# Dilated attention: two units' score products issued in turn from the two halves of the array's rows

## The chip, the cores and the metric

The kernel runs on one core of a Trainium2 chip. The metric is the device time of one execution in microseconds (us). Three runs of the kernel before took 2505.32, 2506.44 and 2511.6 us; the median is 2506.44 us.

## What is computed

The program is two transformer blocks over 512 tokens of width 1024, in float32. The change touches the dilated attention of the second one: three groups of heads (dilations 1, 4 and 16), 16 heads of 64 dimensions each.

```python
proj = (h @ w_in).reshape(B, S, N_GROUPS_2, 3, N_HEADS_2, HEAD_DIM)
for g, (window, dil) in enumerate(DILATED_PATTERNS):      # (128, 1), (512, 4), (2048, 16)
    q = partial_rotary(proj[:, :, g, 0], pos)
    k = partial_rotary(proj[:, :, g, 1], pos)
    v = proj[:, :, g, 2]
    o, lse = dilated_band_attention(q, k, v, dil, window // dil)
...
s = jnp.einsum('bcnihd,bcnjhd->bcnhij', qb, kb).astype(jnp.float32) * (D ** -0.5)
s = jnp.where(valid[None, None, :, None, :, :], s, NEG_INF)
m = jnp.max(s, axis=-1, keepdims=True)
p = jnp.exp(s - m)
den = jnp.sum(p, axis=-1, keepdims=True)
o = jnp.einsum('bcnhij,bcnjhd->bcnihd', p / den, vb.astype(jnp.float32))
```

The three outputs are merged by a softmax over their log-denominators and multiplied by `a_w_out`.

## The kernel before

The mixer is worked through in six passes, `v` = 0 to 5: eight heads of one group each, the groups in the order 1, 2, 0, 1, 2, 0. Tokens are four tiles (`t`) of 128. A **unit** is what fits one PSUM bank of scores, 128 queries by 512 scores: four heads by one key tile in groups 1 and 2 (8 units in a pass), two heads by two key tiles in group 0 (16 units, passes 2 and 5). TensorE does three things for a unit:

- `scores`: four products of 128 x 128, queries by keys, into bank 6 for even units and bank 7 for odd ones. They contract over the 64 dimensions of a head. Even heads lie on partitions 0 to 63 of `dqT` and `dkT` and odd heads on 64 to 127; `first_head` gives all heads of an even unit from the lower half and all of an odd unit from the upper one.
- `turn_probs`: four transposes of the probabilities into bank 4 or 5.
- `times_values`: four products with 64 columns of values, into `G`.

Between them VectorE scales and masks the scores into `dsc` (L2895), reduces the maximum (L2901) and negates it (L2902); ScalarE takes the exponentials (L2115) and copies the transposed probabilities from PSUM to `dPT` (L2103). Both take their work strictly in the order of the code. VectorE also takes a finished tile's output out of `G` (`tile_end`, L2882, or the merge of the three groups in passes 2 and 5) behind its odd units, and rotates the next pass's queries and keys.

In passes 0 to 4 units are laid between the steps of the next pass's projection: `project(v + 1, i)`, i = 0 to 11, each 24 matmuls of 512 columns (L872 to L874), which in turn need weights that ScalarE splits into a high part (L1726) and GpSimd into a low part (L3028). One unit follows each of the steps 1 to 8, or two in group 0 (`units_after`). In pass 5 there is no next projection: one unit lies inside step 11 of its own projection, one behind it, and the others between steps of the output product (`AO_STEPS`), where the first four steps are the transposes at L1417.

A unit is issued as `unit(u)`: `turn_probs(u)`, `scores(u + 2)`, `times_values(u - 1)`, with `scores(0)` and `scores(1)` ahead of the first. `scores(u)` waits until VectorE has read unit `u - 2` (`at_read`), `turn_probs(u)` until its probabilities are there (`at_prob`), `times_values(u)` until ScalarE's copy is (`at_copied`).

Of the kernel before, what the change touches and what calls it, by code (L numbers as in the profile page):

```python
# [28 lines left out]
P = 128  # L29
# [6 lines left out]
DH = 64  # L36
# [53 lines left out]
def two_blocks_kernel(nc, a):  # L90
# [155 lines left out]
    dqT = at("dqT", AR + 16, [P, 4, T])  # L246
# [234 lines left out]
    def first_head(q, heads):  # L481
        return q if heads == 4 else 4 * (q // 2) + q % 2
# [30 lines left out]
    def units_after(v):  # L513
        return [0] + [2 if group_of(v) == 0 else 1] * 8
# [347 lines left out]
    def _(pe):  # L862
# [586 lines left out]
        for v in range(6):  # L1449
            g = group_of(v)  # L1450
            hu = 2 if g == 0 else 4
            per_tile = HH // hu
            units = NT * per_tile

            def scores(u):
                t, q = divmod(u, per_tile)
                if u >= 2:
                    pe.wait_ge(at_read, unit0 - 32 + u - 1)
                for e in range(hu):
                    h = first_head(q, hu) + 2 * e  # L1460
                    rows = slice(DH * (h % 2), DH * (h % 2) + DH)
                    q_ = dqT[rows, h // 2, t * P:(t + 1) * P]
                    keys = ([t, t - 1] if t else [0, 0]) if g == 0 else [t]
                    for z, kt in enumerate(keys):
                        o = (e * len(keys) + z) * P
                        last = pe.matmul(SB[u % 2][:, o:o + P], q_, dkT[rows, h // 2, kt * P:(kt + 1) * P],  # L1466
                                         start=True, stop=True)
                last.then_inc(at_scores, 1)

            def turn_probs(u):  # L1470
                pe.wait_ge(at_prob, unit0 + u + 1)
                if u >= 2:
                    pe.wait_ge(at_copied, unit0 + u - 1)
                for c in range(4):
                    last = pe.transpose(TB[u % 2][:, c * P:(c + 1) * P], dsc[:, u % 3, c * P:(c + 1) * P], ident)
                last.then_inc(at_turned, 1)

            def times_values(u):
                t, q = divmod(u, per_tile)
                pe.wait_ge(at_copied, unit0 + u + 1)  # L1480
                if q == 0:
                    pe.wait_ge(at_done, NT * (v + 1) + t - 1)
                for e in range(hu):
                    h = first_head(q, hu) + 2 * e
                    keys = ([t, t - 1] if t else [0, 0]) if g == 0 else [t]
                    for z, kt in enumerate(keys):
                        o = (e * len(keys) + z) * P
                        last = pe.matmul(G[t % 2][:, h * DH:(h + 1) * DH], dPT[:, u % 3, o:o + P],  # L1488
                                         dV[:, v % 2, kt, h * DH:(h + 1) * DH], start=(z == 0), stop=(z == len(keys) - 1))
                if q == per_tile - 1:  # L1490
                    last.then_inc(at_out, 1)

            def unit(u):
                turn_probs(u)
                if u + 2 < units:
                    scores(u + 2)
                if u >= 1:
                    times_values(u - 1)

            if v < 5:  # L1500
                project(v + 1, 0)
            if v < 5:
                pe.wait_ge(turn_free, chunk[0])
                pe.wait_ge(dl_evac, 12 * (v + 1))
            else:

                pe.wait_ge(turn_free, chunk[0] - 2)
                pe.wait_ge(dl_evac, 12 * (v + 1) - 2)
            scores(0)
            scores(1)  # L1510
            u = 0
            if v < 5:
                for i in range(1, 9):
                    project(v + 1, i)
                    for _ in range(units_after(v)[i]):
                        unit(u)
                        u += 1

                def values_end():
                    times_values(units - 1)  # L1520
                    pe.wait_ge(at_copied, unit0 + units)
                project_values(v + 1, 9, values_end)
            else:
                def first_unit():
                    pe.wait_ge(turn_free, chunk[0])
                    unit(0)

                project(v, 11, first_unit)
                unit(1)
                pe.wait_ge(dl_evac, 12 * (v + 1))  # L1530
                for u in range(2, units):
                    first = sum(AO_STEPS[:u])
                    for f, k in ao_steps[first:first + AO_STEPS[u]]:
                        out_step(f, k)
                    unit(u)
                rest = ao_steps[sum(AO_STEPS):]
                for f, k in rest[:4]:
                    out_step(f, k)
                times_values(units - 1)
                for f, k in rest[4:]:  # L1540
                    out_step(f, k)
            unit0 += units
# [1681 lines left out]
```

## Time and profile before

| | |
|---|---|
| median of three runs | 2506.44 us |
| span of the profiled execution | 2509.7 us |
| TensorE busy | 2449.8 us, 98% of the span |
| VectorE, ScalarE, GpSimd busy | 39%, 39%, 36% |
| granted TensorE clock, mean of the span | 0.993 |
| the six passes, in the trace | 870 to 1437 us |

The span is the time from the first to the last instruction of one profiled execution; no separate time of that execution is shown, and its span lies inside the range of the three runs. Busy time of TensorE counts records of matmuls, which overlap, so 98% says that it seldom waits, not that it works at its peak.

### The profile page before, as it was taken

How to read it: one execution, taken by the hardware profiler on the slowest of the kernel's cores; microseconds unless marked ns; L12 is line 12 of the kernel's file. 1: busy time of each engine (PE TensorE's matmuls, PEld its weight loads, DVE VectorE, ACT ScalarE, POOL GpSimd, SP SyncE). 2: the span in 40 equal slices, each digit the busy share in tenths (PEclk: the TensorE clock that was granted, in tenths of full speed). 3: DMA queues.
4: the chain of work that ended last, by engine and by line, in shares of the span. 5: the costliest groups of instructions: out<-in, count | busy, mean ns of one | idle time of the engine just before them, and what ended most of it. 6: DMA issues, size and time to landing. Idle time of an engine off the chain costs nothing.

```text
span 2509.7 us, 31117 instructions
## 1 busy us (share of the span) xinstructions
PE 2449.8 (98%) x11644; PEld 1930.5 (77%) x11644; DVE 984.9 (39%) x1627; ACT 974.6 (39%) x1611; POOL 906.0 (36%) x757
## 2 busy tenths in 40 slices
PE   7999999999998999999999999999999999999998
PEld 6776786545556998899987878888777777788887
DVE  3276445878884233353335621111311113211113
ACT  3343433656653343343343442222343343422223
POOL 4442141424432433323332154455332221544552
PEclk9999999999999999999999999999999999999999
DMA  5421136899982423311223123323322111233322
GB/s 172 164 67 51 34 125 243 320 380 390 383 321 101 151 70 104 98 51 52 84 91 96 34 84 102 101 94 90 101 102 68 67 51 34 84 101 101 100 85 92
DMA packets 210220, 316.17 MB, mean 126 GB/s; under 512 B 20624, under 2 KB 140176, under 8 KB 200256
## 3 DMA queue, kind: packets, MB, share of 16 engines
q1 hardware_dynamic: 202368, 301.89, 35.4%
q0 software_dynamic: 7744, 12.76, 1.5%
q8 instruction: 76, 1.25, 0.2%
q14 instruction: 32, 0.26, 0.0%
HBM read 300.81 MB, written 22.71 MB: 129 GB/s over the span
## 4 chain that ended last, share of the span: by engine, by line
PE 85%; issue 4%; ACT 3%; DMA 3%; DVE 2%; POOL 2%; SPq 0%; DVEq 0%; ACTq 0%; POOLq 0%
PE bank L872 21%; PE bank L874 20%; PE bank L873 20%; PE bank L1309 4%; PE bank L1102 3%; DMA w_ring<-in_w_gate 2%; PE bank L1466 2%; POOL w_low L3028 2%; PE bank L1488 2%; PE bank L1122 2%; PE bank L1293 2%; PE bank L1288 2%; PE bank L911 2%; ACT w_high L1726 1%; PE bank L1112 1%
## 5 line engine op out<-in xcount | busy, mean ns | idle before, releaser
L3028 POOL TENSOR_TENSOR w_low<-raw,w_high 128x512 fp32r<-128x512 f32 x568 | 748.0, 1349 | 1268.4 <-ACT w_high L1726 1236.5
L872 PE MATMUL bank<-h_high,w_high 128*128 128x512 f32 x1088 | 434.6, 399 | 2.3 <-DVE h_low L2293 2.3
L874 PE MATMUL bank<-h_high,w_low 128*128 128x512 f32 x1088 | 424.6, 390 | 0.0
L873 PE MATMUL bank<-h_low,w_high 128*128 128x512 f32 x1088 | 423.9, 390 | 0.0
L1726 ACT ACTIVATE w_high<-raw 128x2048 fp32r<-128x2048 f32 x145 | 277.0, 1910 | 295.6 <-PE bank L874 283.1
L872 PE MATMUL bank<-w_high,h_high 128*128 128x512 f32 (+2 forms) x832 | 332.5, 400 | 10.6 <-ACT qk L2061 5.5
L874 PE MATMUL bank<-w_high,h_low 128*128 128x512 f32 (+2 forms) x832 | 312.6, 376 | 0.0
L873 PE MATMUL bank<-w_low,h_high 128*128 128x512 f32 (+2 forms) x832 | 312.3, 375 | 0.0
L872 PEld LDWEIGHTS bank<-h_high,w_high 128*128 128x128 f32 x1088 | 204.4, 188 | 50.3 <-DVE h_low L2293 6.1
L874 PEld LDWEIGHTS bank<-h_high,w_low 128*128 128x128 f32 x1088 | 204.2, 188 | 43.5
L873 PEld LDWEIGHTS bank<-h_low,w_high 128*128 128x128 f32 x1088 | 204.6, 188 | 38.9
L872 PEld LDWEIGHTS bank<-w_high,h_high 128*128 128x128 f32 x832 | 205.3, 247 | 26.2 <-ACT qk L2061 5.8
L873 PEld LDWEIGHTS bank<-w_low,h_high 128*128 128x128 f32 x832 | 206.6, 248 | 10.5
L874 PEld LDWEIGHTS bank<-w_high,h_low 128*128 128x128 f32 x832 | 204.9, 246 | 12.6
L2545 DVE TENSOR_TENSOR up_low<-w_ring,up_high 128x2048 fp32r<-128x2048 f32 x70 | 160.1, 2288 | 39.2 <-ACT up_high L1980 36.9
L2276 DVE TENSOR_TENSOR X<-bank,X 128x512 f32<-128x512 f32 x96 | 65.8, 690 | 235.6 <-PE bank L874 235.4
L2273 DVE TENSOR_TENSOR gu<-silu,bank 128x512 f32<-128x512 f32 x44 | 30.3, 688 | 321.4 <-ACT silu L2173 321.4
L2173 ACT ACTIVATE silu<-bank 128x512 f32<-128x512 f32 x44 | 26.3, 599 | 333.0 <-PE bank L874 333.0
L1980 ACT ACTIVATE up_high<-w_ring 128x2048 fp32r<-128x2048 f32 x70 | 133.9, 1915 | 33.3 <-DMA w_ring<-in_w_gate 30.7
L872 PE MATMUL bank<-w_high,act_high 128*128 128x512 f32 x352 | 136.9, 389 | 0.0
L873 PE MATMUL bank<-w_low,act_high 128*128 128x512 f32 x352 | 136.9, 389 | 0.0
L874 PE MATMUL bank<-w_high,act_low 128*128 128x512 f32 x352 | 136.9, 389 | 0.0
(374 smaller groups left out, 3501.7 us busy)
## 6 DMA issues: line engine op xcount, KB each, us to landing
raw<-in_ffn_w_gu SPq DMA_DIRECT2D x88, 512.0 KB, 4.5
raw<-in_a_w_in SPq DMA_DIRECT2D x72, 512.0 KB, 4.8
w_ring<-in_w_gate SPq DMA_DIRECT2D x35, 1024.0 KB
w_ring<-in_w_up SPq DMA_DIRECT2D x35, 1024.0 KB
w_ring<-in_w_down SPq DMA_DIRECT2D x35, 1024.0 KB
raw<-in_ffn_w_down SPq DMA_DIRECT2D x40, 512.0 KB, 4.6
raw<-in_w_in SPq DMA_DIRECT2D x34, 512.0 KB, 4.7
raw<-in_b_w_in SPq DMA_DIRECT2D x24, 512.0 KB, 4.8
```

Source lines behind the costliest of these rows:

```text
L872: pe.matmul(out, sta[0], mov[0], start=start, stop=False)
L873: pe.matmul(out, sta[0], mov[1], start=False, stop=False)
L874: return pe.matmul(out, sta[1], mov[0], start=False, stop=stop)
L911: last = pe.transpose(TB[m % 2][:, t * P:(t + 1) * P], src, ident)
L1102: pe.matmul(S3[u % deep][:, 0:(qt + 1) * P], q_[rows, h // 2, qt * P:(qt + 1) * P], k_[rows, h // 2, 0:(qt + 1) * P], start=True, stop=False)
L1122: last = pe.matmul(G[qt % 2][:, h * DH:(h + 1) * DH], pt_[:, u % deep, kt * P:(kt + 1) * P], v_[:, kt, h * DH:(h + 1) * DH], start=(kt == ...
L1309: last = pe.matmul(G[2 + half][0:R, :], het[:, c, :], w[:, c, 512 * half:512 * half + 512], start=(c == 0), stop=(c == 1))
L1726: act.activation(w_high[:, slot, :], raw[:, slot, :], ACT.Copy).then_inc(high_done, 1)
L1980: act.activation(up_high[:, b, :, FE * q:FE * q + FE], ring[:, q, :].rearrange("p (k n) -> p k n", k=KD), ACT.Copy).then_inc(m_high, 1)
L2276: return dve.tensor_tensor(out=out, in0=x, in1=y, op=ALU.add)
L2545: dve.tensor_tensor(out=up_low[:, b, :, FE * q:FE * q + FE], in0=ring[:, q, :].rearrange("p (k n) -> p k n", k=KD), in1=up_high[:, b, :, F ...
L3028: last = pool.tensor_tensor(out=w_low[:, slot, cols], in0=raw[:, slot, cols], in1=w_high[:, slot, cols].bitcast(F32), op=ALU.subtract)
```

## The change

Units are taken by twos. `scores(u)`, now for even `u` only, issues the eight products of units `u` and `u + 1` in turn: one of the even unit (lower half of the rows, bank 6), one of the odd unit (upper half, bank 7), and so on, and waits for both units before. `pair(u)` is two `turn_probs`, the eight score products of the next two units, and two `times_values`, that of `u - 1` and, new in its place, that of `u`. In passes with one unit after each projection step the pair follows every second step. The work of the other engines and its order are the same.

```diff
             def scores(u):
-                t, q = divmod(u, per_tile)
                 if u >= 2:
-                    pe.wait_ge(at_read, unit0 - 32 + u - 1)
-                for e in range(hu):
-                    h = first_head(q, hu) + 2 * e
-                    rows = slice(DH * (h % 2), DH * (h % 2) + DH)
-                    q_ = dqT[rows, h // 2, t * P:(t + 1) * P]
-                    keys = ([t, t - 1] if t else [0, 0]) if g == 0 else [t]
-                    for z, kt in enumerate(keys):
-                        o = (e * len(keys) + z) * P
-                        last = pe.matmul(SB[u % 2][:, o:o + P], q_, dkT[rows, h // 2, kt * P:(kt + 1) * P],
-                                         start=True, stop=True)
-                last.then_inc(at_scores, 1)
+                    pe.wait_ge(at_read, unit0 - 32 + u)
+                for i in range(4):
+                    for w in (u, u + 1):
+                        t, q = divmod(w, per_tile)
+                        keys = ([t, t - 1] if t else [0, 0]) if g == 0 else [t]
+                        e, z = divmod(i, len(keys))
+                        h = first_head(q, hu) + 2 * e
+                        rows = slice(DH * (h % 2), DH * (h % 2) + DH)
+                        last = pe.matmul(SB[w % 2][:, i * P:(i + 1) * P], dqT[rows, h // 2, t * P:(t + 1) * P],
+                                         dkT[rows, h // 2, keys[z] * P:(keys[z] + 1) * P], start=True, stop=True)
+                        if i == 3:
+                            last.then_inc(at_scores, 1)
...
-            def unit(u):
+            def pair(u):
                 turn_probs(u)
+                turn_probs(u + 1)
                 if u + 2 < units:
                     scores(u + 2)
                 if u >= 1:
                     times_values(u - 1)
+                times_values(u)
...
-                    for _ in range(units_after(v)[i]):
-                        unit(u)
-                        u += 1
+                    u = sum(units_after(v)[:i + 1])
+                    if u % 2 == 0:
+                        pair(u - 2)
...
-                def first_unit():
+                def first_units():
                     pe.wait_ge(turn_free, chunk[0])
-                    unit(0)
-
-                project(v, 11, first_unit)
-                unit(1)
+                    pair(0)
+
+                project(v, 11, first_units)
                 pe.wait_ge(dl_evac, 12 * (v + 1))
-                for u in range(2, units):
+                for u in range(2, units, 2):
                     first = sum(AO_STEPS[:u])
-                    for f, k in ao_steps[first:first + AO_STEPS[u]]:
+                    for f, k in ao_steps[first:first + AO_STEPS[u] + AO_STEPS[u + 1]]:
                         out_step(f, k)
-                    unit(u)
+                    pair(u)
```

On TensorE, in pass 2 behind projection step 2, the rows before are these. Banks 4 and 5 take the turned probabilities (`dsc`), 6 and 7 the scores (`dkT`, `dqT`), 0 and 1 are `G`.

```order
L1475 MATMUL bank4<-cst_50,dsc_184 128x128 x4
L1466 MATMUL bank6<-dkT_180,dqT_179 128x128 x4
L1488 MATMUL bank0<-dV_182,dPT_185 128x64 x4
L1475 MATMUL bank5<-cst_50,dsc_184 128x128 x4
L1466 MATMUL bank7<-dkT_180,dqT_179 128x128 x4
L1488 MATMUL bank0<-dV_182,dPT_185 128x64 x4
```

In the change the same place reads so (the lines have moved by one).

```order
L1476 MATMUL bank4<-cst_50,dsc_184 128x128 x4
L1476 MATMUL bank5<-cst_50,dsc_184 128x128 x4
L1466 MATMUL bank6<-dkT_180,dqT_179 128x128
L1466 MATMUL bank7<-dkT_180,dqT_179 128x128
L1466 MATMUL bank6<-dkT_180,dqT_179 128x128
L1466 MATMUL bank7<-dkT_180,dqT_179 128x128
L1466 MATMUL bank6<-dkT_180,dqT_179 128x128
L1466 MATMUL bank7<-dkT_180,dqT_179 128x128
L1466 MATMUL bank6<-dkT_180,dqT_179 128x128
L1466 MATMUL bank7<-dkT_180,dqT_179 128x128
L1489 MATMUL bank0<-dV_182,dPT_185 128x64 x8
```

The number of products is the same; six runs of one kind of work have become three, and banks 6 and 7 alternate.

The second place is in pass 5 on TensorE, behind projection step 11: the rows before, from unit 1 to unit 3, with the transposes of the output product (L1417) between them.

```order
L1475 MATMUL bank5<-cst_50,dsc_184 128x128 x4
L1466 MATMUL bank7<-dkT_180,dqT_179 128x128 x4
L1488 MATMUL bank0<-dV_182,dPT_185 128x64 x4
L1417 MATMUL bank2<-cst_50,xn_92 128x128 x4
L1417 MATMUL bank3<-cst_50,xn_92 128x128 x4
L1475 MATMUL bank4<-cst_50,dsc_184 128x128 x4
L1466 MATMUL bank6<-dkT_180,dqT_179 128x128 x4
L1488 MATMUL bank0<-dV_182,dPT_185 128x64 x4
L1417 MATMUL bank2<-cst_50,xn_92 128x128 x4
L1417 MATMUL bank3<-cst_50,xn_92 128x128 x4
L1475 MATMUL bank5<-cst_50,dsc_184 128x128 x4
L1466 MATMUL bank7<-dkT_180,dqT_179 128x128 x4
```

And in the change, from the last matmul of step 11:

```order
L874 MATMUL bank3<-w_high_88,h_low_91 128x512
L1417 MATMUL bank2<-cst_50,xn_92 128x128 x4
L1417 MATMUL bank3<-cst_50,xn_92 128x128 x4
L1417 MATMUL bank2<-cst_50,xn_92 128x128 x4
L1417 MATMUL bank3<-cst_50,xn_92 128x128 x4
L1476 MATMUL bank4<-cst_50,dsc_184 128x128 x4
L1476 MATMUL bank5<-cst_50,dsc_184 128x128 x4
L1466 MATMUL bank6<-dkT_180,dqT_179 128x128
L1466 MATMUL bank7<-dkT_180,dqT_179 128x128
```

Unit 1 has moved ahead, into the middle of step 11; no unit stands between step 11 and the transposes, nor between the first and the second two of them.

## Rows read from the trace of the kernel before

**Rows 1.** The page, busy time and share of each engine.

```profile
PE 2449.8 (98%) x11644; PEld 1930.5 (77%) x11644; DVE 984.9 (39%) x1627; ACT 974.6 (39%) x1611; POOL 906.0 (36%) x757
```

**Rows 2.** Passes 2 and 5: busy us (instructions) of each engine, granted clock, DMA.

```profile
1054.00:1168.00 114.00, 114.00 (x643) 108.65 (x643) 60.28 (x113) 45.09 (x102) 31.36 (x25) 1.00 0.21 65
...
1339.00:1437.00 98.00, 93.68 (x552) 78.39 (x550) 61.98 (x116) 38.35 (x97) 19.96 (x16) 0.97 0.19 55
```

**Rows 3.** Score line L1466 by source: ns min/median/max; idle us, times.

```profile
L1466 PE MATMUL bank<-dkT,dqT x512: 272/272/579, 871.1 to 1420.9; 64*128 64x128 f32 x171
...
  issue: 10.2, 57
```

**Rows 4.** Timeline, TensorE, pass 0: start us, us, work; one unit between projection steps.

```profile
894.42 0.60 PE L1475 MATMUL bank<-cst,dsc 128*128 128x128 f32 x4
894.95 1.16 PE L1466 MATMUL bank<-dkT,dqT 64*128 64x128 f32 x8
896.04 1.10 PE L1488 MATMUL bank<-dV,dPT 128*128 128x64 f32 x8
896.95 0.60 PE L872 MATMUL bank<-w_high,h_high 128*128 128x512 f32 x1
897.39 0.40 PE L873 MATMUL bank<-w_low,h_high 128*128 128x512 f32 x1
897.63 0.40 PE L874 MATMUL bank<-w_high,h_low 128*128 128x512 f32 x1
```

**Rows 5.** Timeline, TensorE, pass 2: two units next to each other.

```profile
1072.29 0.60 PE L1475 MATMUL bank<-cst,dsc 128*128 128x128 f32 x4
...
1077.82 0.40 PE L873 MATMUL bank<-w_low,h_high 128*128 128x512 f32 x1
```

**Rows 6.** Timeline, pass 1, scores 0 and 1 next to each other: loads and products.

```profile
964.27 1.52 PEld L1466 LDWEIGHTS bank<-dkT,dqT 64*128 64x128 f32 x16 [0.35 <-issue]
964.27 1.71 PE L1466 MATMUL bank<-dkT,dqT 64*128 64x128 f32 x16
```

**Rows 7.** Timeline, TensorE, pass 1: one unit between projection steps.

```profile
978.71 0.60 PE L1475 MATMUL bank<-cst,dsc 128*128 128x128 f32 x4
...
981.56 0.39 PE L873 MATMUL bank<-w_low,h_high 128*128 128x512 f32 x1
```

**Rows 8.** Timeline, pass 0: end of step 7, rotation, GpSimd's low part, start of step 9.

```profile
927.68 0.40 PE L874 MATMUL bank<-w_high,h_low 128*128 128x512 f32 x1
...
930.00 2.52 DVE L2273 TENSOR_TENSOR rot<-qk,cst 128x256 f32<-128x256 f32 x4
...
930.69 5.82 POOL L3028 TENSOR_TENSOR w_low<-raw,w_high 128x512 fp32r<-128x512 f32 x4 [3.92 <-ACT w_high L1726]
...
933.88 1.51 DVE L2276 TENSOR_TENSOR qk<-rot 128x256 f32<-128x256 f32 x1
...
936.57 0.63 PE L872 MATMUL bank<-w_high,h_high 128*128 128x512 f32 x1
```

**Rows 9.** Timeline, start of pass 5: turning of unit 0, last exponential of unit 1, turning of unit 3.

```profile
1347.29 0.63 PE L1475 MATMUL bank<-cst,dsc 128*128 128x128 f32 x4 [0.57 <-ACT dsc L2115]
...
1348.07 0.49 ACT L2115 ACTIVATE dsc<-dsc,nmx 128x256 f32<-128x256 f32 x1
...
1360.98 0.66 PE L1475 MATMUL bank<-cst,dsc 128*128 128x128 f32 x4 [2.12 <-ACT dsc L2115]
```

**Rows 10.** Windows, columns as in rows 2: a stretch of pass 5.

```profile
1361.60:1368.40 6.80, 6.80 (x24) 5.93 (x24) 3.18 (x8) 2.47 (x8) 0.00 (x0) 0.50 0.49 154
```

**Rows 11.** Timeline, pass 2: values of unit 3, GpSimd, last exponential of unit 7.

```profile
1084.84 1.10 PE L1488 MATMUL bank<-dV,dPT 128*128 128x64 f32 x8
...
1086.47 5.47 POOL L3028 TENSOR_TENSOR w_low<-raw,w_high 128x512 fp32r<-128x512 f32 x4 [6.04 <-ACT w_high L1726]
...
1092.77 0.50 ACT L2115 ACTIVATE dsc<-dsc,nmx 128x256 f32<-128x256 f32 x1
```

**Rows 12.** Timeline, VectorE, pass 5: a finished output group is added.

```profile
1369.77 0.69 DVE L2276 TENSOR_TENSOR X<-bank,X 128x512 f32<-128x512 f32 x1 [4.53 <-PE bank L874]
```

More of the change, by code:

```diff
@@ L1509, in _ @@
             scores(0)
-            scores(1)
-            u = 0
             if v < 5:
```

## The prediction, made before the changed kernel ran

> **What bounds the kernel now.** I read the page first: TensorE is busy for 98% of the span and every other engine for less than 40% [rows 1], so only time on TensorE counts, unless the change makes it wait. The windows say the same of the passes: in pass 2 it is busy for all 114 us at a clock of 1.00, with VectorE at 60 and ScalarE at 45 us; pass 5 has 4 us of waiting and a clock of 0.97 [rows 2]. The timeline then gives a unit's price. A matmul of 512 columns follows the last one after 0.24 us (897.39 to 897.63), and a unit is what lies between two of them beyond that: in pass 0 it is 897.39 − 894.42 − 0.24 = 2.73 us, in pass 1 981.56 − 978.71 − 0.23 = 2.62 [rows 4, 7]; two next to each other cost 1077.82 − 1072.29 − 0.24 = 5.29 [rows 5].
>
> Inside a unit every product of scores or values stands twice in the records (512 for 256, [rows 3]). Eight records of scores last 1.16 us with 0.27 for a single one, so they start (1.16 − 0.27) / 8 = 0.11 us apart; the eight of values take 0.91 us until the next matmul, also 0.11 each, though they have half the columns; four transposes take 0.44 [rows 3, 4]. Ahead of the scores stands a gap of about 0.2 us that nothing released: the source view counts 57 of them, 10.2 us, and there are 58 runs of scores (64 units, of which the first two of each of six passes make one run); the same again is seen between scores and values (last score record starting at about 895.84, values at 896.04) [rows 3, 4].
>
> The row that decides is the start of a pass, where scores 0 (lower half) and 1 (upper half) stand next to each other. Sixteen records end after 1.71 us, where 1.16 + 8 × 0.11 = 2.05 would be serial: 0.34 us or three places were shared by the two halves, for loads of the stationary operand too (1.52 us for sixteen) [rows 6]. So the halves do run at the same time, each at its own 0.11, as far as the engine sees past what is queued: here about three products of the lower half.
>
> **The change, part by part.** *Sharing.* With the halves in turn the other half is never more than two records away, so I take all eight places as shared: eight products of two units cost what four do. Bounds: nothing shared, 0 us, or 8 × 0.11 = 0.89 us for each two units; the row is at three of eight only because the lower half had its run first, and I take the upper end.
>
> The Trainium skill (TensorE: Matmul & The Clock Gate, Part 3, The mechanism) says that loads overlap matmuls of another row group but that matmuls start and end strictly in program order. By that the halves would still share, but each run would end one place later, 0.11 us, 3.5 us over the 32 runs. The trace does not agree with a strict order: by it the upper half in rows 6 could share one place, not three, and sixteen records would end at 1.94 us and not at 1.71 [rows 6]. So I don't subtract it.
>
> *Fewer turns between kinds of work.* Two units together have one run of scores instead of two, so two gaps of 0.2 us less, and in passes of one unit a step one return to the 512-column matmuls less (872 to 873 takes 0.44 instead of 0.24 us [rows 4], 0.2; about 0.1 in pass 1). Put together, a full pair is one unit plus four transposes and eight value records: 2.73 + 0.44 + 0.89 = 4.06 us in passes 0, 2 and 3; 2.62 + 1.33 = 3.95 in 1, 4 and 5.
>
> The sum on TensorE, without waits:
> - passes 0 and 3: first scores 0.45 (five more places shared, less what rows 6 have: 5 × 0.11 is 0.55, of which the start of the second half keeps 0.1); first pair, where unit 0 had no values, 1.4; two full pairs at 2 × 2.73 − 4.06 = 1.4; last pair 0.5. The last pair is where step 9 now waits for GpSimd's low part: step 7 ends at 927.68, step 9 starts at 936.57, 8.89 us later, and the low part ends 8.83 later [rows 8]. Without the wait the change needs 5.64 for step 8, 0.24, and 2.54 for the pair: 8.42; GpSimd's 5.8 us, which overlap VectorE's rotation before, are nearer 5.0 when the rotation comes later. 5.1 us a pass, 10.3.
> - passes 1 and 4: 0.45 + 1.3 + 2 × 1.3 + 0.6 = 4.95, 9.9 for both.
> - pass 2: 0.45 + 1.2 + 6 × (5.29 − 4.06 = 1.23) + 0 for the last = 9.1.
> - pass 5: five full pairs at 1.3 = 6.5; the start apart.
>
> *New waits.* The order of the code lets a pair ask for its second unit's probabilities 0.44 us behind the first's; so far there was a step between them. Behind them on TensorE's queue stand the next scores, for which VectorE waits. In pass 2 one step (24 × 0.235 = 5.64 us) lies between. The longest chain starts where `tile_end` takes values of the tile out: values of unit 3 end at 1085.94, unit 7's last exponential at 1093.27, 7.3 us later, with GpSimd's low part beside it [rows 11]. In the pair those values end 3.4 us behind the step's last matmul, so the probabilities are there at 10.7, and are asked for at 4.06 + 5.64 + 0.44 = 10.1: 0.6 late, at two of the three tile ends, where GpSimd runs, and 0.1 elsewhere. 1.4 us, 7.7 are left of pass 2.
>
> In passes 0, 1, 3 and 4 two steps lie between, so the second unit is asked for at 15.8 where that chain ends at 10.7; one pair of a pass has a rotation in it too, 5.4 us at its longest, beside GpSimd (930.00 to 935.39) [rows 8], which would bring it to 16.1, but GpSimd is idle there. Nothing, and 0.3 us a pass if not; each further us late would be a us of TensorE.
>
> In pass 5 VectorE adds a finished output group ahead of the odd unit's scores [rows 12]; that group now ends half way between two pairs, at 4.06 + 12 × 0.235 + 0.3 = 7.2 us, the add takes 0.6, and the unit is two such operations and a short one on VectorE (1.6 us) and two exponentials of 0.50 on ScalarE (1.0) [rows 11, 12], which gives 10.4 for 10.1: 0.3 in each of four pairs, 1.25.
>
> *Start of pass 5.* Unit 1 moves into the middle of step 11. Its exponentials end at 1348.56 [rows 9], so turning it starts at 1348.8 instead of following at 1347.7: 1.1 us. Then all of unit 1's work comes before the second half of the step, the transposes (L1417) wait for ScalarE's copy of the last tile (an estimate of 0.7 + 0.4 us, as long as an operation of VectorE on 512 columns [rows 12]), and the third of them waits for VectorE, which waits for ScalarE, which has unit 2's exponentials, a copy and a split of 1.9 us ahead. Followed in the code's order, unit 3 is turned at about 1363.9 where it was 1360.98 [rows 9]; with the runs saved since, the first four output steps end 0.75 us later than they do now, if the clock is as good. It isn't good now: 1361.6 to 1368.4 ran at 0.50 [rows 10]. There will be more waiting ahead of it (some 5 us for 2.1), so I take such a stretch as given, under scores and values instead of partly under steps: 2.2 us more. Together a loss of 3, between 0 and 4.
>
> The waits for values cost nothing: ScalarE's copy of the pair's first unit (0.6 us) ends under the second transposes and the scores, 2 us ahead of need. The wait for two units' reading costs nothing either; VectorE has read both before their exponentials.
>
> Sum: 10.3 + 9.9 + 7.7 + 6.5 − 1.25 − 3 = 30.1 us of the span of 2509.7. The span is 0.13% above the median of the runs, which I correct for by taking the difference from the median: 2506.4 − 30.1 = **2476 us**.
>
> **Rivals.**
> - *No sharing* when the halves alternate, only the fewer turns. 26 full or first pairs lose 0.89 each and six first scores 0.45: 30.1 − 23.1 − 2.7 = 4.3 us of gain, 2502, no change that can be told. For it: a product is two records of one half, and rows 6 show runs, not alternation. Against: those rows show both loads and products shared. 0.07.
> - *The chain behind is later than I follow it*: VectorE slower beside GpSimd, so that each of the twelve pairs of passes 2 and 5 waits another 1 us. 12 us back: 2488. For it, the margins there are below 1 us; against, the other four passes have 4 us and more. 0.12.
> - *The clock falls* in the pairs, the other side. A stretch such as rows 10's is 6.8 us at half speed and costs at most 3.4. To end 7.5 us slower it takes (30.1 + 7.5) / 3.4 = 11 more, one for every third pair: 2514. For it, the one stretch in these passes came where TensorE had small work and 2 us of waiting; against, rows 5's two units, 5.3 us of small work, longer than a pair, and their like in all of pass 2, are at 1.00 [rows 2, 5]. 0.04. The Trainium skill (the same page, Part 4, PE-mode transpose) has it that transposes don't count as activity for the clock, and a pair has eight in a row; no row separates them from the other small work.
>
> **How the numbers follow.** My forecast has 0.75, and its own range is 2467 (no waits, no stretch at half clock) to 2484. No sharing 0.07, chain 0.12, clock 0.04, and 0.02 for something else slower. 2467 to 2489 takes in the chain's case and leaves less than 0.2 out. A change of 0.3%, 7.5 us, is about what a measurement of this kernel can tell from none. Faster is the forecast, the chain's case and little of the rest, 0.87; same 0.07; slower 0.06.
>
> **What the profile will show.** Sixteen score records in about 1.2 us, with 32 such runs and some 32 gaps instead of 57; an insertion of about 4.06 us in pass 2 for 5.29, and 3.95 in pass 1; step 9 of pass 0 no later than 8.9 us behind step 7; waits on L1476 for ScalarE of 0.1 to 0.6 us in pass 2 and of 2 us or more at the start of pass 5, with a clock of 0.50 near 1355 to 1365. Runs of 2 us for sixteen records would make the prediction wrong by 23 us, and waits of over 1 us in most pairs of pass 2 by the half of it.

## The result, and the profile after

The change takes 2486.7 us (median of four runs, 2485.99 to 2488.2) where the kernel before takes 2507.27 beside it (four runs): ratio 0.9915, 95% interval 0.9901 to 0.9929. The time lies 10.7 us above the forecast of 2476 and 2.7 above the forecast's own range of 2467 to 2484; it is inside the wide range, up to 2489, that takes in the case of a later chain. The profiled execution has a span of 2484.2 us, 25.5 less than the one before, and a time of its own of 2485.99.

The page, its span and the busy time of each engine [rows 1 before]:

```profile
span 2484.2 us, 31117 instructions
...
PE 2419.0 (97%) x11644; PEld 1905.2 (77%) x11644; DVE 967.8 (39%) x1627; ACT 972.5 (39%) x1611; POOL 911.0 (37%) x757
```

TensorE is busy for 31 us less, with the same 11644 instructions: records that lie on top of others, and fewer turns between kinds of work, which count as busy too. Of those, 25.5 are left in the span, so some waiting is new. The source view of the score line says the first part directly [rows 3]:

```profile
L1466 PE MATMUL bank<-dkT,dqT x512: 272/272/580, 869.4 to 1393.4; 64*128 64x128 f32 x171
...
  issue: 6.0, 31
```

The records last as long as before, 272 ns; the gaps ahead of a run of scores fell from 57 with 10.2 us to 31 with 6.0. The timeline of TensorE in pass 2 shows a full pair [rows 5]:

```profile
1058.61 0.40 PE L874 MATMUL bank<-w_high,h_low 128*128 128x512 f32 x1
1058.85 1.03 PE L1476 MATMUL bank<-cst,dsc 128*128 128x128 f32 x8
1059.81 1.16 PE L1466 MATMUL bank<-dkT,dqT 64*128 64x128 f32 x16
1060.90 2.00 PE L1489 MATMUL bank<-dV,dPT 128*128 128x64 f32 x16
1062.71 0.61 PE L872 MATMUL bank<-w_high,h_high 128*128 128x512 f32 x1
1063.16 0.40 PE L873 MATMUL bank<-w_low,h_high 128*128 128x512 f32 x1
```

Sixteen score records end after 1.16 us, exactly what eight took in [rows 4], and the pair takes 1063.16 − 1058.85 − 0.24 = 4.07 us; the prediction had 4.06. All 32 runs are of sixteen; thirty take 1.16 us, the other two, at a clock of 0.50, 1.61 and 2.08.

The windows give passes 2 and 5 and two stretches of pass 5 (PE busy, loads, VectorE, ScalarE, GpSimd, granted clock, DMA) [rows 2, 10]:

```profile
1050.50:1155.50 105.00, 104.97 (x641) 101.32 (x640) 58.75 (x113) 44.38 (x103) 31.07 (x24) 1.00 0.19 61
1309.40:1410.00 100.60, 86.66 (x543) 71.46 (x541) 59.27 (x114) 38.18 (x97) 19.97 (x16) 0.93 0.18 54
1319.50:1326.30 6.80, 6.80 (x30) 5.71 (x27) 1.55 (x3) 0.00 (x0) 0.00 (x0) 0.50 0.84 233
1333.20:1340.00 6.80, 5.49 (x33) 4.53 (x31) 3.65 (x7) 2.54 (x7) 2.88 (x3) 0.50 0.38 117
```

Pass 2 is full to the last 0.03 us at full clock. Pass 5 is idle for 14 us of 100.6, where it was idle for 4.3 of 98, and its clock is 0.93 for 0.97. The waits of TensorE in pass 5 (total us, times, longest) name who ends that idle time:

```profile
PE bank L1476 <- ACT dsc L2115: 5.4, 7, 1.4
PE bank L1417 <- DVE h_low L2279: 3.4, 1, 3.4
PE bank L872 <- DVE X L2276: 1.7, 2, 0.8
PE bank L872 <- DVE h_low L2279: 1.3, 1, 1.3
PE bank L872 <- POOL w_low L3028: 0.9, 1, 0.9
PE bank L1417 <- ACT dV L2061: 0.8, 1, 0.8
PE bank L911 <- DVE dkT L2819: 0.4, 1, 0.4
```

To compare whole passes, each is taken from the last matmul of 512 columns ahead of its first scores to that of the next pass, and pass 5 to the first such matmul behind its last values. All runs below are put into this table (us; the sum is of passes 0 to 4):

| kernel | 0 | 1 | 2 | 3 | 4 | sum | 5 |
|---|---|---|---|---|---|---|---|
| before | 93.21 | 90.47 | 113.64 | 93.21 | 78.53 | 469.06 | 95.58 |
| the change | 88.04 | 85.65 | 104.94 | 88.04 | 73.67 | 440.34 | 100.50 |
| forecast | 88.1 | 85.5 | 105.9 | 88.1 | 73.6 | 441.2 | 93.3 |
| runs of four | 90.20 | 87.54 | 110.55 | 90.20 | 75.57 | 454.06 | 105.29 |
| same half | 91.58 | 88.88 | 112.11 | 91.58 | 76.91 | 461.06 | 105.99 |
| pass 5 by units | 88.04 | 85.64 | 104.94 | 88.04 | 73.67 | 440.33 | 95.48 |
| only pass 5 | 93.20 | 90.48 | 113.64 | 93.20 | 78.50 | 469.02 | 99.68 |
| the change again | 88.04 | 85.68 | 104.97 | 88.04 | 73.71 | 440.44 | 100.31 |
| clock kept | 88.04 | 85.65 | 104.93 | 88.03 | 73.67 | 440.32 | 95.51 |
| start by units | 88.03 | 85.68 | 104.96 | 88.04 | 73.70 | 440.41 | 93.86 |
| and adds late | 88.03 | 85.68 | 104.95 | 88.04 | 73.70 | 440.40 | 94.25 |
| units, then pairs, kept | 88.04 | 85.65 | 104.93 | 88.04 | 73.69 | 440.35 | 92.29 |
| and adds late to 9 | 88.04 | 85.64 | 104.95 | 88.04 | 73.66 | 440.33 | 93.80 |

A pass repeats from one kernel to another within 0.05 us where nothing in it was changed, and pass 5 within 0.2, with one exception: the change's own pass 5 takes 100.50 and 100.31, but 99.68 in "only pass 5", where the same code has its 13.7 us at half clock in one stretch instead of two. So this table tells tenths apart in passes 0 to 4, and in pass 5 as long as the clock is looked at too, where whole executions of one kernel differ by 2 to 14 us: what lies ahead of pass 0 alone took 868 to 874 us in these traces, without any relation to the edits.

So passes 0 to 4 give 28.7 us, and pass 5 takes 4.9 of them back. What was open: whether the 28.7 come from the two halves or from the fewer turns between kinds of work, and what pass 5 pays for.

### The profile page after: what moved, and what is told of

It is laid out like the page before. It is cut to its first block, busy times and chain, and to the rows that moved or that the text cites. A ratio compares the mean times of both kernels' runs of the same rounds, so it can differ in the third digit from the quotient of the medians.

```text
span 2484.2 us, 31117 instructions
## 1 busy us (share of the span) xinstructions
PE 2419.0 (97%) x11644; PEld 1905.2 (77%) x11644; DVE 967.8 (39%) x1627; ACT 972.5 (39%) x1611; POOL 911.0 (37%) x757
## 3 DMA queue, kind: packets, MB, share of 16 engines
q8 instruction: 76, 1.25, 0.2%
## 4 chain that ended last, share of the span: by engine, by line
PE 86%; issue 4%; ACT 3%; DVE 2%; DMA 2%; POOL 2%; SPq 0%; DVEq 0%; POOLq 0%; ACTq 0%
PE bank L872 21%; PE bank L874 20%; PE bank L873 20%; PE bank L1309 4%; PE bank L1102 3%; PE bank L1293 2%; PE bank L1489 2%; PE bank L1288 2%; PE bank L1122 2%; DMA w_ring<-in_w_gate 2%; POOL w_low L3028 2%; PE bank L911 1%; PE bank L1466 1%; PE bank L1112 1%; ACT w_high L1726 1%
```

## The experiments

**Do the halves share, and does it take the alternation?** Two kernels keep the pairs whole and change the scores alone. The first issues the four products of the even unit, then the four of the odd one:

```diff
-                for i in range(4):
-                    for w in (u, u + 1):
+                for w in (u, u + 1):
+                    for i in range(4):
```

> The changed kernel with one line pair swapped: in scores(u) the loop over the two units is outside and that over the four products inside, so a pair issues four products of the lower half and then four of the upper; everything else, the pairs too, is as in the change. Theory (the gain is the two halves running at once, each at 0.11 us a record, and the engine looks about three records ahead): sixteen records take 1.71 us as in rows 6 instead of 1.16, 0.55 more in each of 32 runs, 17 us, so 2504 us, little faster than before. Rival (the gain is fewer turns between kinds of work): 2487 us as the change, sixteen records near 1.2 us or their length of no effect.

It took 2503.2 us (ratio 0.9978, 0.9969 to 0.9988; ten runs against 27 of before, 2509.97). The second keeps the alternation but reads both units' heads from the lower half of the rows, so that the odd unit's scores are those of the even heads:

```diff
-                        rows = slice(DH * (h % 2), DH * (h % 2) + DH)
+                        rows = slice(0, DH)
```

> The changed kernel with the products still in turn between banks 6 and 7, but both units' operands taken from partitions 0 to 63 (the odd heads' scores are thus computed from the even head beside them, so the output is not the reference's; number, size and order of all instructions are the change's). Theory (sharing needs two different halves of the rows): sixteen records in 2.05 us, 0.89 us more a run, 28 us in 32 runs, 2515 us, slower than before although it has the fewer turns. Rival (alternating banks, or longer runs, is what helps): 2487 us and sixteen records near 1.2 us.

It took 2511.3 us (ratio 1.0005, 0.9992 to 1.0019). The timeline's row of sixteen score records in pass 2 in the first:

```profile
1063.82 1.71 PE L1466 MATMUL bank<-dkT,dqT 64*128 64x128 f32 x16
```

and in the second:

```profile
1057.83 2.05 PE L1466 MATMUL bank<-dkT,dqT 64*128 64x128 f32 x16
```

So the same sixteen records take 2.05 us from one half, 1.71 from both in runs of one unit, 1.16 in turn. Pairs alone, without any sharing, take 469.06 − 461.06 = 8.0 us less than the kernel before in passes 0 to 4; sharing as runs of four have it gives another 7.0, alternation 13.7. There are 24 runs of sixteen in these passes, and 24 × (1.71 − 1.16) = 13.2. The kernel before already shares 0.34 us in the first run of each pass, 1.7 us in five, which the second kernel gives up. So the fewer turns between kinds of work, the rival, have 9.7 of the 28.7 us, and sharing that was not there before has 19.0. Pass 5, with eight such runs, is 4.8 and 5.5 us longer in these two kernels than in the change. 1.71 in every run at full clock, wherever it stands, shows that the three shared places of [rows 6] are no accident of a pass's start.

The Trainium skill (TensorE: Matmul & The Clock Gate, Part 3, The mechanism) keeps matmuls in strict order at start and end. With two records of a product in one half, that would end a run of four and four at 1.94 us and a run in turn one place late, 1.27; measured are 1.71 and 1.16, so this trace does not bear that part out. Single records say it directly: in runs of four, the upper half's first record starts at 1064.375, beside the fifth of the lower half's eight (1064.369) and ahead of its last three. That is two products early; since a run's second record follows its first after 0.21 us instead of 0.11, three records' places are left, 0.34 us. That loads of the other half overlap, the trace does bear out.

**Is it pass 5 alone that loses?** One kernel takes its units in pass 5 by ones again, as before, and keeps the pairs elsewhere; another does the opposite.

```diff
-                for u in range(2, units, 2):
+                for u in range(2, units):
                     first = sum(AO_STEPS[:u])
-                    for f, k in ao_steps[first:first + AO_STEPS[u] + AO_STEPS[u + 1]]:
+                    for f, k in ao_steps[first:first + AO_STEPS[u]]:
                         out_step(f, k)
-                    pair(u)
+                    unit(u)
```

> Passes 0 to 4 by pairs as in the change, pass 5 by single units in the order of before. Theory (the profile of the change: passes 0 to 4 gained 28.7 us together, pass 5 lost 4.9): pass 5 takes 94.4 us again, the whole 4.9 us less than the change, 2482 us, with one stretch at half clock in pass 5 instead of two. Rival (pass 5's loss is the luck of one execution's clock): no difference from the change, 2487 us.

```diff
-                    u = sum(units_after(v)[:i + 1])
-                    if u % 2 == 0:
-                        pair(u - 2)
+                    for _ in range(units_after(v)[i]):
+                        unit(u)
+                        u += 1
```

> The other way round: passes 0 to 4 by single units as before, pass 5 by pairs as in the change. Theory: 4.9 us slower than before, 2512 us, with the change's waits at the start of pass 5 (some 3.4 us at L1417). Rival (the pairs gain in pass 5 too and the loss was the clock of one execution): 2507 us or less, down to 2501.

2482.56 us (0.9890, 0.9876 to 0.9904) and 2515.38 us (1.0020, 1.0011 to 1.0030). By the table, pairs in pass 5 alone cost 4.1 us and units in it give 5.0 back; passes 0 to 4 don't notice. The parts add up within the 0.8 us by which the change's pass 5 itself differs, and in pass 5 the change is a loss.

**What does pass 5 pay for?** The timeline of its start in the change (us, duration, engine and line; in brackets the idle time ahead and what ended it) [rows 9]:

```profile
1316.89 0.63 PE L1476 MATMUL bank<-cst,dsc 128*128 128x128 f32 x4 [1.08 <-ACT dsc L2115]
1318.32 0.66 PE L1476 MATMUL bank<-cst,dsc 128*128 128x128 f32 x4 [0.79 <-ACT dsc L2115]
1318.90 1.61 PE L1466 MATMUL bank<-dkT,dqT 64*128 64x128 f32 x16
1320.44 1.97 PE L1489 MATMUL bank<-dV,dPT 128*128 128x64 f32 x8
1327.86 1.09 PE L1417 MATMUL bank<-cst,xn 128*128 128x128 f32 x8 [0.78 <-ACT dV L2061]
1332.33 1.58 PE L1417 MATMUL bank<-cst,xn 128*128 128x128 f32 x8 [3.38 <-DVE h_low L2279]
1333.70 1.06 PE L1476 MATMUL bank<-cst,dsc 128*128 128x128 f32 x4
1336.07 1.11 PE L1476 MATMUL bank<-cst,dsc 128*128 128x128 f32 x4 [1.31 <-ACT dsc L2115]
1337.11 2.08 PE L1466 MATMUL bank<-dkT,dqT 64*128 64x128 f32 x16
```

It waits for units 0 and 1, works at half clock from 1319.5 on, waits again for 0.78 and 3.38 us and has its second stretch at half clock from 1333.2. I repeated the change and put beside it a kernel that issues matmuls of 512 columns (one call: of 256) into a bank that is free (`keep_clock`) at these waits, and changes no order and no operand of the rest:

```diff
                 def first_units():
                     pe.wait_ge(turn_free, chunk[0])
-                    pair(0)
+                    keep_clock(1, G[1], 256)
+                    turn_probs(0)
+                    keep_clock(1, G[1])
+                    turn_probs(1)
+                    scores(2)
+                    times_values(0)
...
+                        if u == 2 and f == 0:
+                            keep_clock(1, G[1])
+                        if u == 2 and f == 2:
+                            keep_clock(4, G[1])
                         out_step(f, k)
+                    if u == 2:
+                        keep_clock(1, G[1])
                     pair(u)
```

> The changed kernel itself, timed beside the next three. Both theories: 2487 us. Whether its pass 5 again has two stretches at half clock says if they belong to the order of the code (theory: 100.5 us in pass 5 again) or to chance (rival: between 95 and 101).

> The change with idle work for TensorE in the waits at the start of pass 5: matmuls into bank 1, which nothing uses then, one of 256 columns ahead of turning unit 0, one of 512 ahead of unit 1, one ahead of the first transposes of the output product, four ahead of the third, one ahead of pair 2. Theory (both the waits and the clock that falls in them cost): the waits stay, the two stretches at half clock go and with them 5 us, 2481 to 2482 us. Rival (the clock falls because of small work, not of waiting, or its stretches lie in waits anyway): no gain, 2487 us.

The change again took 2488.34 us (0.9916, 0.9902 to 0.9929; before 2510.41), the kernel with the filler 2483.67 (0.9901, 0.9886 to 0.9917). Whole times hardly separate the two, their intervals overlap. The granted clock of all their executions does, 0.992 to 0.993 in five of the change, 0.994 to 0.996 in four with the filler. So do the profiles: the change again has two stretches of 6.8 us at half clock, as the theory had it, and the window of pass 5 with the filler has none:

```profile
1309.97:1405.48 95.51, 87.00 (x558) 69.59 (x556) 59.20 (x114) 38.18 (x97) 19.99 (x16) 1.00 0.20 56
```

The clock is 1.00 and the pass takes 95.5 us for 100.3: half clock costs 4.8 us here, of two stretches of 6.8. The waits that remain are the same but for those filled; the one for `dV` remains too, since its filler (L901) stands behind it:

```profile
PE bank L1476 <- ACT dsc L2126: 3.4, 6, 1.4
PE bank L872 <- DVE X L2287: 1.7, 2, 0.8
PE bank L872 <- DVE h_low L2290: 1.3, 1, 1.3
PE bank L872 <- POOL w_low L3039: 0.9, 1, 0.9
PE bank L901 <- ACT dV L2072: 0.8, 1, 0.8
PE bank L911 <- DVE dkT L2830: 0.4, 1, 0.4
```

With the clock out of the way, pass 5 is still no better than before, 95.51 for 95.58, where five full pairs should have been worth 6 us. The next kernel takes units 0 to 3 by ones as before, and pairs from unit 4:

```diff
+                for u in range(2, 4):
+                    first = sum(AO_STEPS[:u])
+                    for f, k in ao_steps[first:first + AO_STEPS[u]]:
+                        out_step(f, k)
+                    unit(u)
-                for u in range(2, units, 2):
+                for u in range(4, units, 2):
```

> Passes 0 to 4 by pairs; in pass 5 units 0 to 3 one by one as before, pairs from unit 4. Theory (the loss of pass 5 is in its start, 7 us, and the later pairs gain little because VectorE adds the output groups ahead of the odd unit): pass 5 takes 95.3 us, the whole 2482 us, as with all of pass 5 by units. Rival (the later pairs are worth 1.2 us each as in pass 2, and only the start lost): 2477 us.

2483.42 us (0.9898, 0.9883 to 0.9913), pass 5 in 93.86: between the two. The loss at the start is gone, and 1.6 us more. That looks like a gain of the later pairs, and is none. Pass 5 can be parted where the first four output steps behind unit 3 end, at their last 512-column matmul: in the kernels of this table all time at half clock lies ahead of it, and all the later pairs lie behind it. That matmul in the kernel before, the change, this kernel and the last but one of this section:

```profile
1369.34 0.39 PE L874 MATMUL bank<-w_high,h_low 128*128 128x512 f32 x1
1343.91 0.39 PE L874 MATMUL bank<-w_high,h_low 128*128 128x512 f32 x1
1337.41 0.39 PE L874 MATMUL bank<-w_high,h_low 128*128 128x512 f32 x1
1337.67 0.39 PE L874 MATMUL bank<-w_high,h_low 128*128 128x512 f32 x1
```

| kernel | start of pass 5 to there, us | of it at half clock | from there to the end |
|---|---|---|---|
| before | 29.55 | 6.8 | 66.03 |
| pass 5 by units | 29.45 | 6.8 | 66.03 |
| the change | 34.51 | 13.7 | 65.99 |
| clock kept | 29.63 | 0 | 65.88 |
| start by units | 27.96 | 3.4 | 65.90 |
| units, then pairs, kept | 26.37 | 0 | 65.92 |

Behind that point every kernel takes 65.9 to 66.0 us, by units or by pairs: the five later pairs together are worth 0.1 us. The 1.6 us are the clock. This execution has 3.4 us at half clock where "by units" and the kernel before have 6.8, though the code up to there is theirs; what decides between the two lengths no run shows. So the theory was right on the pairs, and its 95.3 us were missed through the clock.

In the trace the pairs at units 4 and 6 take 4.59 us from the last 512-column matmul ahead to the first behind, and those at 10 and 12, with no wait, 4.10. The idle time shown ahead of the second unit's transposes is only 0.27, but the distance grows by 0.49: records of transposes last 0.27 us and normally start 0.11 apart, and idle time is counted only behind the end of a record. To see why the later pairs gain nothing, and whether VectorE's addition of finished groups makes the odd units late, as the prediction has it, I moved the additions of units 4 to 13 behind the odd unit's scores, on VectorE and in ScalarE's part of the same work:

```diff
+                late = v == 5 and 4 <= u < 14
+                if late and u % 2:
+                    for f in ao_groups[u - 1] + ao_groups[u]:
+                        after_group(f)
...
-                    for f in ao_groups[u]:
+                    for f in () if late else ao_groups[u]:
```

> As start_by_units, and for units 4 to 13 of pass 5 ScalarE and VectorE take the output groups of two units together, after the odd unit and ahead of the tile's end and of the copy for TensorE, instead of after each unit. Theory (the later pairs wait for the odd unit, held up by the add of a group that ends half way): its waits on ScalarE go, each pair gets 0.9 to 1.2 us back, pass 5 takes 90 to 91 us, 2477 us. Rival (the waits behind it are those for weights and for the banks of the output groups, which stay): 2482 us.

2483.67 us (0.9900, 0.9885 to 0.9916), 94.25 us for pass 5: no gain. Yet the pairs at 4, 6 and 8 are 4.09, 4.10 and 4.49 long now instead of 4.58, 4.59 and 6.06: the waits for the additions are gone. The waits say where it went:

```profile
PE bank L1476 <- ACT dsc L2147: 4.0, 3, 2.1
PE bank L872 <- DVE h_low L2315: 3.4, 1, 3.4
PE bank L872 <- DVE X L2312: 1.2, 2, 0.9
```

The turned output of tile 0, which a later output step multiplies, is split on VectorE by the same code that I moved. TensorE was 2.6 us ahead of the kernel beside it when it came there (56.64 us into the pass for 59.23); it lost 2.1 of them to this wait, which had been 1.3 us, and 1.6 to a stretch of 3.4 us at half clock behind it (the next 2.6 us of matmuls took 4.2). The cause of the pairs' waits is shown; the remedy moved the loss.

**Both remedies together.** The last two kernels start by units, with the first scores in turn, and fill 1.8 us of the 2.1 us that unit 3's turning waits; the second of them also moves the additions, but only up to unit 9.

```diff
+                    if u == 3:
+                        keep_clock(2, G[1])
                     unit(u)
```

```diff
-                late = v == 5 and 4 <= u < 14
+                late = v == 5 and 4 <= u < 10
```

> Pass 5 takes units 0 to 3 one at a time and the others in pairs, its first two units' scores are issued in turn (as in the change), and two matmuls that only keep the clock fill 1.8 us of the 2.1 us wait ahead of unit 3. Theory (the loss at the start of pass 5 is its clock and its waits): the 3.4 us at half level near 1333 of the run without the filler go, worth up to 1.7 us, and sixteen score records end 0.5 us earlier: pass 5 in 91.7 to 92.8 us (93.86 without these two edits), 2481 to 2482.5 us. Rival (the filler delays unit 3's turning by what it saves): 93.5 to 94.5 us, no gain.

> The kernel before it, with VectorE's addition of a finished output group moved behind the odd unit's scores for units 4 to 9 only, so that tile 0's turned output (whose low part held step after unit 10 up by 3.4 us when it was moved too) keeps its place. If the later pairs' waits for ScalarE come from those additions: 0.45 us less in each of the pairs at units 4, 6 and 8 and no new wait of 3.4 us, together 1 to 1.5 us less than the kernel beside it, 90.3 to 91.7 us in pass 5. If the chain is late for another reason, or the wait of L872 for VectorE comes again: no difference, or up to 2 us more.

2479.48 us (0.9869, 0.9852 to 0.9885; before 2511.13) and 2478.57 (0.9870, 0.9854 to 0.9887), each four runs; the first is ahead of the change by more than both intervals. Its wait for unit 3 is down to 0.41 us, and no stretch of pass 5 is at half clock:

```profile
1330.17 1.88 PE L901 MATMUL bank<-cst 128*128 128x512 f32 x4
1332.46 0.66 PE L1476 MATMUL bank<-cst,dsc 128*128 128x128 f32 x4 [0.41 <-ACT dsc L2145]
1333.05 1.16 PE L1514 MATMUL bank<-dkT,dqT 64*128 64x128 f32 x8
```

92.29 us are 1.57 less than without the filler and the first scores in turn, and 8.2 less than the change. All of the 1.57 lies in the start (26.37 for 27.96 in the table above), where 3.4 us at half clock are gone. The sharing of the first scores, which the theory counted with 0.5, gave nothing: their run is 0.55 us shorter, but turning unit 0 starts 7.49 us into the pass in both kernels and waits 1.11 us instead of 0.57. Of the 8.2, 3.3 are the order of the start (29.63 − 26.37, both at full clock) and 4.9 the clock. Units in all of pass 5 with the same filler were not run; by the table they would take 26.4 + 66.0 = 92.4 us, an estimate, so the pairs have no part in this gain. In the second kernel the pairs at 4, 6 and 8 are 4.10, 4.10 and 4.49 long, as hoped, but pass 5 takes 1.5 us more. Its waits:

```profile
PE bank L1476 <- ACT dsc L2145: 2.8, 3, 1.4
PE bank L872 <- DVE h_low L2313: 2.3, 1, 2.3
```

TensorE is again 2.6 us ahead (55.07 for 57.64), but the turned tile 0 comes only 1.6 earlier, so the wait for `h_low` is 2.3 instead of 1.3. Behind it lies a stretch of 3.4 us at half clock (near 1367), which takes the remaining 1.6: at unit 10 both kernels are 61.9 us into the pass. The last 1.5 us go with a second such stretch near 1398. My expectation fell, by the wait and by the clock that followed it. A version with filler in this wait too wasn't made.

## Why the prediction was right, and where it was not

The direction, the sharing and passes 0 to 4 came as forecast. That the time lies in the wide range is in part luck: pass 5 missed by 7.2 us, and the range reaches to 2489 for waits in passes 2 and 5 that came in pass 5 alone.

**Sharing: right.** All eight places are shared: 1.16 us, and 4.07 for a full pair. The "three products" that the prediction read from rows 6 are three records, one and a half products. 24 runs at 2.05 − 1.16 = 0.89 make 21.4; same half and the change differ by 20.7 in passes 0 to 4.

**Fewer turns: right.** For the kernel "same half" the prediction's sum gives 27.9 − 24 × 0.89 = 6.5 us with the waits in pass 2 taken off, 7.9 without; measured are 8.0.

**Passes 0, 1, 3, 4: right**, 5.17, 4.82, 5.17 and 4.86 for 5.1 and 4.95. Step 9 of pass 0 waits for GpSimd's low part in the kernel before and, as reckoned, no longer in the change. GpSimd and the start of step 9 in the change, where step 7 ends at 921.29:

```profile
924.30 5.00 POOL L3028 TENSOR_TENSOR w_low<-raw,w_high 128x512 fp32r<-128x512 f32 x4 [4.34 <-ACT w_high L1726]
...
929.75 0.61 PE L872 MATMUL bank<-w_high,h_high 128*128 128x512 f32 x1
```

The low part takes 5.00 us instead of 5.82 and ends 8.01 us behind step 7; step 9 starts 8.46 behind it, for 8.42 in the sum and 8.89 before [rows 8].

**Waits in pass 2: mis-sized.** I took 1.4 us off; the profile shows no wait at L1476 in passes 0 to 4, and of the full pairs of pass 2 one is longer, by 0.25 us (units 6 and 7, at the first tile end). The pass gained 8.7 for 7.7, and 9.1 without waits (its terms add up to 9.0). At that tile end the probabilities are there 10.4 us behind the step's last matmul for 10.7 reckoned, and are asked for at 10.4 for 10.1; at the second they are there 1.3 us early.

**Later pairs of pass 5: the step that failed most.** The prediction gave five full pairs 6.5 us and took 1.25 off for waits, 5.25. From the end of the first four output steps to the end of the pass they gave 66.03 − 65.99 = 0.04 us, 0.15 with the clock kept. An undisturbed pair saves 2 × 2.76 − 4.10 − 0.24 = 1.18 for 1.3, 0.6 in five. The odd units' waits were taken as 0.3 in four pairs; three pairs have 0.49. But a late VectorE also makes the output steps wait, which the sum hadn't: twice 0.8 for a bank that it has yet to add (`X`), and 1.3 for the turned tile 0 (`h_low`). GpSimd's low part adds 0.9 once, and turning unit 15 waits 1.4 where its values waited 1.2 before. 0.6 + 1.5 + 1.7 + 1.3 + 0.9 + 0.2 = 6.2 us, where 1.25 were taken off; 0.3 of the missing 6.5 stay open.

**Start of pass 5: mis-sized, by the clock.** The prediction reckoned that turning unit 3 would start at 1363.9, that is 24.1 us into the pass, and that the first four output steps would end 0.75 us later than before at a good clock; one stretch at half clock was charged with 2.2 us, 3 in all "between 0 and 4". With the clock kept, turning unit 3 starts 23.5 us into the pass (1333.49 − 1309.97) and the four steps end at 29.63 for 29.55, 0.1 later, so the chain was followed well. In the change turning starts 26.7 in (1336.07 − 1309.40) and the steps end at 34.51: a loss of 5.0 where 3 was reckoned. The term that was mis-sized is the clock: there are two stretches of 6.8 us instead of one, worth 4.9 us and not 2.2. The rows that could have told were there: 2.12 us of waiting stood ahead of one such stretch in [rows 9, 10], and the prediction itself put some 5 us of waiting where there had been 2.1 (measured: 1.08 + 0.79 + 0.78 + 3.38 + 1.31 = 7.3). Where the waits more than doubled, I kept one stretch. The comparison with before also hides something: its own stretch costs it 3.2 us (29.55 for 26.37), so at full clock on both sides the order of the pairs loses 3.3 us in this start.

**Rivals.** No sharing fell with the rows of 1.16. "The chain behind is later" had its place in passes 2 and 5; in pass 2 it came to 0.25 us, in pass 5 it came in part, and its 2488 is close to the result by another sum. "The clock falls" came true in pass 5 only: two stretches, not eleven. What the Trainium skill says of transposes and the clock (TensorE: Matmul & The Clock Gate, Part 4, PE-mode transpose), quoted there, had no effect that a row shows: 24 pairs in passes 0 to 4, each with eight in a row, ran at full clock.

**The absolute number.** The span was to be 2509.7 − 30.1 = 2479.6 and is 2484.2: 7.2 more in pass 5 (5.2 of it the later pairs, 2.0 the start), 0.8 less in passes 0 to 4, 1.7 less ahead of pass 0. The other 6 us between 2476 and 2486.7 aren't the change's: I took the difference from the median of three runs, 2506.4, which is 3.3 below the span that the sum was made against; 1.8 lie between a span and its time; the median is 0.7 above the profiled execution. Beside the later kernels the one before took 2509.97, 2510.41 and 2511.13: the low median was chance, and the trace's own time was the better base.

## What to carry to other kernels

Products that contract over 64 rows belong in turn on the two halves, product by product: that was worth 0.89 us for each sixteen records against one half and 0.55 against runs of four. When work is gathered into larger pieces, look at the place where the pieces have least cover, here a start with 7 us of waits; count what the clock does at each wait, not once, and try leaving that place as it was. When two kernels differ, see where the time between them lies before it is put down to an edit: 1.6 us in pass 5 looked like the pairs' and were the clock's. A unit that is asked for earlier makes the engine behind it late for everything else in its queue, so follow that queue to its next customer too.

## What the runs showed of the hardware

The two halves overlap for loads and products: by three records of 128 columns, 0.34 us, when each half has a run of eight, by all eight when they alternate by product. Each half stays at 0.11 us a record in all cases.

Ahead of products over half the rows stands a gap of about 0.2 us each time (6.0 us in 31 gaps). From values to transposes, both over all rows, the next record starts after 0.11 us like any other. The Trainium skill (TensorEngine Tiling (Array Packing), Key Properties) says that changing the tiling mode drains TensorE; the rows agree.

A wait between four and four transposes that the profile shows as 0.27 us moved what follows by 0.49: the fifth starts 0.55 us behind the fourth instead of 0.11, of which 0.27 are the fourth's own record.

Matmuls that compute nothing can pay: 3.6 us of filler in the 3.4 us wait, and 3.8 at the four smaller ones, shortened pass 5 by 4.8 us: without them the granted clock was at 0.50, its level of 1.2 GHz, for 13.7 us, with them it was at 1.00, 2.4 GHz, throughout. In the start by units 1.9 us of filler in one wait of 2.1 us left no stretch where there had been one of 3.4 us, worth 1.6.
